# Waits of two output projections taken per pair, and two weight chunks summed earlier, in a two-block transformer kernel on one core

## The reference

```python
# first block
merged = jnp.einsum('bsnd,nbsd->bsd', gates, branch)
x = x + merged @ w_out[layer]                      # output projection, 512x1024 @ 1024x1024
# second block
h = rms_norm_2(x, norm_mix[l])
proj = h @ w_in[l]                                 # input projection, 6 strips of 392 columns, and gates
u, q, kc, vc, ksl, vsl, kwn, vwn, g_nsa, g_merge = jnp.split(proj, IN_SPLITS, axis=-1)
...                                                # compress(kc), compress(vc), pooling, sparse attention
merged = g_a * (y_pool @ w_proj_pool[l]) + g_b * (y_nsa @ w_proj_nsa[l])
x = x + merged @ w_out[l]                          # output projection
h = rms_norm_2(x, norm_mlp[l])
x = x + jnp.square(jax.nn.relu(h @ w_ff1[l])) @ w_ff2[l]
```

## Time and profile before

| | before |
|---|---|
| median of 3 runs | 1459.08 us (1457.42 to 1463.24) |
| profiled execution, own time | 1459.08 us |
| its span | 1457.3 us |
| PE busy | 1421.2 us, 98% |
| PE weight load busy | 1187.6 us, 81% |
| DVE / ACT / POOL busy | 61% / 46% / 42% |
| granted TensorE clock, mean | 0.998 |
| DMA | 170.30 MB, mean 117 GB/s |

### The profile page before, as it was taken

One profiled execution on the slowest core, in us unless ns is written; L12 is line 12 of the kernel. 1 busy time (PEld: TensorE's weight loads), 2 busy tenths in 40 slices (PEclk: granted clock), 3 DMA queues, 4 the chain that ended last, 5 costly groups with the idle time before them and its releaser, 6 DMA issues.

```text
span 1457.3 us, 20968 instructions
## 1 busy us (share of the span) xinstructions
PE 1421.2 (98%) x7693; PEld 1187.6 (81%) x7693; DVE 882.9 (61%) x1646; ACT 665.8 (46%) x1176; POOL 616.1 (42%) x433
## 2 busy tenths in 40 slices
PE   8999999989989999999999999999999999999998
PEld 7888888768778888889997777788888888888886
DVE  4336978465654276652555777772164777777776
ACT  5453645557564233343343666773235433223342
POOL 4333744344343445254433265563425333333330
PEclk9999999999999999999999999999999999999999
DMA  6222433203101666769662210004365433333321
GB/s 207 83 83 84 143 95 98 60 12 93 44 2 48 205 203 233 267 197 325 232 235 73 73 30 1 2 2 145 98 215 179 159 102 101 101 101 104 97 86 58
DMA packets 89115, 170.30 MB, mean 117 GB/s; under 512 B 7032, under 2 KB 31171, under 8 KB 89027
## 3 DMA queue, kind: packets, MB, share of 16 engines
q1 hardware_dynamic: 79298, 140.72, 30.7%
q10 hardware_dynamic: 9728, 28.39, 5.4%
HBM read 148.12 MB, written 20.97 MB: 116 GB/s over the span
## 4 chain that ended last, share of the span: by engine, by line
PE 91%; DVE 3%; ACT 2%; issue 2%; DMA 1%; POOL 1%; POOLq 0%; SPq 0%; DVEq 0%; ACTq 0%
PE bank L1015 58%; PE bank L1700 9%; PE bank L1276 4%; PE bank L1077 4%; PE bank L1284 4%; PE bank L1107 4%; PE bank L938 3%; PE bank L975 1%; PE bank L1109 1%; PE bank L1688 1%; DVE xt_lo L2953 1%; PE bank L1518 0%; PE bank L1227 0%; DMA raw<-in_w_in 0%; DVE prob_t L2765 0%
## 5 line engine op out<-in xcount | busy, mean ns | idle before, releaser
L774 POOL TENSOR_TENSOR w_lo<-raw,w_hi 128x1024 fp32r<-128x1024 f32 (+3 forms) x185 | 439.5, 2386 | 496.0 <-ACT w_hi L1776 495.7
L1776 ACT ACTIVATE w_hi<-raw 128x1024 fp32r<-128x1024 f32 (+3 forms) x189 | 191.4, 1015 | 367.5 <-DMA raw<-in_w_in 175.0
L1015 PE MATMUL bank<-xt_hi,w_hi 128*128 128x512 f32 x560 | 221.2, 395 | 0.0
L1015 PE MATMUL bank<-xt_hi,w_lo 128*128 128x512 f32 x560 | 218.2, 390 | 0.0
L1015 PE MATMUL bank<-xt_lo,w_hi 128*128 128x512 f32 x560 | 218.1, 389 | 0.0
L1015 PE MATMUL bank<-w_hi,xt_hi 128*128 128x484 f32 (+2 forms) x520 | 192.1, 369 | 0.0
L1015 PE MATMUL bank<-w_lo,xt_hi 128*128 128x484 f32 (+2 forms) x520 | 190.2, 366 | 0.0
L1015 PE MATMUL bank<-w_hi,xt_lo 128*128 128x484 f32 (+2 forms) x520 | 190.1, 366 | 0.0
L1015 PEld LDWEIGHTS bank<-xt_hi,w_hi 128*128 128x128 f32 x560 | 105.2, 188 | 23.4 <-issue 2.2
L1015 PEld LDWEIGHTS bank<-xt_hi,w_lo 128*128 128x128 f32 x560 | 105.1, 188 | 22.2
L1015 PEld LDWEIGHTS bank<-xt_lo,w_hi 128*128 128x128 f32 x560 | 105.2, 188 | 21.6 <-issue 0.5
(11 more groups left out here) (453 smaller groups left out, 2957.9 us busy)
## 6 DMA issues: line engine op xcount, KB each, us to landing
raw<-in_w_in SPq DMA_DIRECT2D x40, 512.0 KB, 3.6
raw<-in_w_in SPq DMA_DIRECT2D x40, 484.0 KB, 3.5
raw<-in_w_ff SPq DMA_DIRECT2D x36, 512.0 KB, 3.7
quarter_b<-in_w_ff SPq DMA_DIRECT2D x28, 512.0 KB, 3.5
raw<-in_w_in SPq DMA_DIRECT2D x24, 392.0 KB, 3.8
w_hi<-sums_hi SPq DMA_DIRECT2D x16, 512.0 KB, 4.9
w_lo<-sums_lo SPq DMA_DIRECT2D x16, 512.0 KB, 5.8
raw<-in_w_branch SPq DMA_DIRECT2D x12, 512.0 KB, 3.8
```

Source lines behind the costliest of these rows:

```text
L774: pool.tensor_tensor(w_lo[:, slot, 0:halves, 0:width], raw[:, slot, 0:halves, 0:width], w_hi[:, slot, 0:halves, 0:width].bitcast(F32), ALU ...
L1015: ins = pe.matmul(o, lhs, rhs, start=st and j == 0, stop=en and j == 2)
L1776: act.activation(w_hi[:, slot, 0:halves, 0:width], raw[:, slot, 0:halves, 0:width], ACT.Copy)\
```

## The change

Two edits.

In `out_products` the three terms of a pair are written inside the loops over its two row blocks and two banks. All waits of the pair stand ahead of its first matmul: both parts of the weights, both parts of the activations. `high_made`, `low_made`, `high_landed` and `low_landed` become `wait_pair` and `wait_sums`.

In the second block's input projection the steps of the chunks 5, 6 and 7 are moved. On ACT the high part and the stores of chunk 5 come before `empty_in2(2)`, those of chunk 6 before `empty_in2(3)`, the load of 7 before `next_hi(I + 21)`, and its high part behind `hidden_turned`. On DVE chunk 5 comes before the groups `ck` and `cv`, and chunk 6 before the gate signals.

```diff
@@ out_products
-                        for j, (rows, whole) in enumerate(((rows_hi, w_hi), (rows_lo, w_hi), (rows_hi, w_lo))):
-                            if j == 0:
-                                high_landed(p) if m in OF_SUMS else high_made(p)
-                            if j < 2 and m in (1, 4):
-                                pe.wait_ge(sem[("mhi", "mlo")[j]], 4 * n + (m == 4) * 2 + q + 1)
-                            if j < 2 and m in S_ORDER:
-                                pe.wait_ge(sem[("sums_hi", "sums_lo")[j]], 4 * n + S_ORDER.index(m) + 1)
-                            if j == 2:
-                                low_landed(p) if m in OF_SUMS else low_made(p)
-                            for kk in range(2):
-                                for u in range(2):
...
+                        if m in OF_SUMS:
+                            wait_sums(p)
+                        else:
+                            wait_pair(p)
+                        if m in (1, 4):
+                            pe.wait_ge(sem["mhi"], 4 * n + (m == 4) * 2 + q + 1)
+                            pe.wait_ge(sem["mlo"], 4 * n + (m == 4) * 2 + q + 1)
+                        for kk in range(2):
+                            wh, wl = w_hi[:, p % RING, kk, :], w_lo[:, p % RING, kk, :]
+                            for u in range(2):
+                                c = slice(u * P, u * P + P)
+                                lh, ll = rows_hi[:, 2 * q + kk, c], rows_lo[:, 2 * q + kk, c]
+                                for j, (lhs, rhs) in enumerate(((lh, wh), (lh, wl), (ll, wh))):
+                                    ins = pe.matmul(bank[OUT_BANK[m] + u][:], lhs, rhs,
...
@@ ACT, input projection of the second block
             for q in range(11, 15):
                 next_hi(I + q, IN2_W)
+                if q in (12, 13):
+                    (chunk_high if q == 12 else chunk_store)(5)
             empty_in2(2)
...
-            chunk_high(5)
             next_hi(I + 15, IN2_W)
+            chunk_load(6)
...
+            for q in range(16, 19):
+                next_hi(I + q, IN2_W)
+                if q in (17, 18):
+                    (chunk_high if q == 17 else chunk_store)(6)
             empty_in2(3)
             next_hi(I + 19, IN2_W)
             next_hi(I + 20, IN2_W)
-            chunk_high(6)
-            chunk_store(6)
+            chunk_load(7)
             next_hi(I + 21, IN2_W)
             hidden_tanh()
-            chunk_load(7)
...
             next_hi(I + 23, IN2_W)
+            hidden_turned()
             chunk_high(7)
-            hidden_turned()
@@ DVE
             whole_chunk(4)
+            whole_chunk(5)
             for k, (name, pe_col) in enumerate((("ck", VEC["pek"]), ("cv", VEC["pev"]))):
...
-            whole_chunk(5)
...
+            whole_chunk(6)
             dve.wait_ge(sem["tanh_out"], 1)
...
-            whole_chunk(6)
```

More of the change, by code:

```diff
@@ L1037, in turn_x, with wait_sums @@
                     .then_inc(sem["x_turned"], 1)
-            def high_landed(p):
-                pe.wait_ge(landed[p % RING], p // RING * 16 + 16)
-            def low_landed(p):
-                pe.wait_ge(landed_lo[p % RING], 16 * sum(t <= p and t % RING == p % RING for t in SUM_PAIRS))
+            def wait_sums(p):
+                slot = p % RING
+                pe.wait_ge(landed[slot], p // RING * 16 + 16)
+                pe.wait_ge(landed_lo[slot], 16 * sum(t <= p and t % RING == slot for t in SUM_PAIRS))
             def out_products(n, s, p0):
@@ L1057, in out_products @@
                     if m in S_ORDER:
+                        pe.wait_ge(sem["sums_hi"], 4 * n + S_ORDER.index(m) + 1)
+                        pe.wait_ge(sem["sums_lo"], 4 * n + S_ORDER.index(m) + 1)
                         k = S_ORDER.index(m)
@@ L1064, in out_products @@
                         p = p0 + 2 * i + q
-                        slot = p % RING
-                        for j, (rows, whole) in enumerate(((rows_hi, w_hi), (rows_lo, w_hi), (rows_hi, w_lo))):
-                            if j == 0:
-                                high_landed(p) if m in OF_SUMS else high_made(p)
-                            if j < 2 and m in (1, 4):
-                                pe.wait_ge(sem[("mhi", "mlo")[j]], 4 * n + (m == 4) * 2 + q + 1)
-                            if j < 2 and m in S_ORDER:
-                                pe.wait_ge(sem[("sums_hi", "sums_lo")[j]], 4 * n + S_ORDER.index(m) + 1)
-                            if j == 2:
-                                low_landed(p) if m in OF_SUMS else low_made(p)
-                            for kk in range(2):
-                                for u in range(2):
-                                    ins = pe.matmul(bank[OUT_BANK[m] + u][:], rows[:, 2 * q + kk, u * P:u * P + P], whole[:, slot, kk, :],
+                        if m in OF_SUMS:
[12 more added lines that the diff above has]
+                                    ins = pe.matmul(bank[OUT_BANK[m] + u][:], lhs, rhs,
                                                     start=m in (1, 7, 4, 6) and q == 0 and kk == 0 and j == 0,
```

11 lines of the change are left out of this document (1 added, 10 removed).

## The result

The changed kernel takes 1469.28 us (median of 8 runs, 1465.67 to 1470.86), the kernel before 1461.65 (8 runs beside it, 1457.42 to 1465.42). The ratio is 1.0052 with a 95% interval of 1.0038 to 1.0067: **slower by 0.5%**, 5.6 to 9.8 us. Forecast were 1464.9 us and 5.8 us of loss, with a range up to 1469.0: the direction held, the loss is larger, and the time lies just outside the range.

The account below looks back on a forecast made before the run. PE was taken to bound the kernel. Projections 1.1, chunk 5 standstill 3.6, clock 1.4, strip 3 stores 0 and gate strip -0.3 sum to 5.8 us on 1459.08, giving 1464.9 us; range 1461 to 1469.

Parts of the forecast that it names:

- What bounds the kernel: Whole kernel: PE is busy 98% of the span, so each microsecond PE stands still is a microsecond of time.
- Product 2: Both output projections: PE waits for POOL's low part of the weights, 0.7 us in the first, 0.4 in the second.
- Loads of sums: Output projections: loads awaited at the head of their pair still land in time, by 0.7 us; cost nothing.
- Chunk 5 ahead of the groups: Before strip 3: DVE finishes groups ck and cv at 700.2, PE comes at 696.62; 3.6 us of standstill.
- my allowance for the landing: Chunk 5's loads: a microsecond allowed for the landing, giving 2.6 us of standstill at the short end.
- The collision: Chunk 5's fourth add on DVE meets POOL's pair 12 low part: all 1.5 us later, 1466.4 us; chance 0.20.
- The clock: Behind the standstill at strip 3: PE's granted clock falls, costing 1.4 us, bounds nothing and 2.8.
- the rival without a fall: Strip 3: the clock doesn't fall, everything else as forecast, 1463.5 us; chance 0.22.
- Strip 3 behind the stores of chunk 6: ACT empties strip 3 after those stores: costed at nothing; rival 1.6 us more, 1466.5 us, chance 0.06.
- Gate strip: PE's 1.14 us wait at 760.90 may shrink: -0.3 us, between -1.1 and +0.5.
- Pay-back: PE's later waits, 760 to 850 us, shrink by up to 4.0 us and the clock stays: 1459.8 us; chance 0.07.
- The base: Starting time: the profiled execution's 1459.08 us, taken also as the median of the runs.

Follow-up runs that it names:

- e2: Kernel before with only the moved chunk steps on ACT and DVE, products as before: 1468.46 us, ratio 1.0042.
- e8: Kernel before with only chunk 7's loads ahead of pair 21's high part and the hidden layer turned ahead of chunk 7's high part: 1459.26 us, ratio 0.9985.
- e10: e7 with chunk 5's loads issued one pair earlier on ACT: 1462.72 us, ratio 1.0016 against the kernel before.
- e11: e8 with chunk 5's loads issued one pair earlier: 1459.41 us, ratio 0.9986 against the kernel before.
- e13: Kernel before, unchanged, profiled once more: 1462.79 us.
- e15: Kernel before, unchanged, another profile: 1458.97 us.
- e5: e2 with 18 extra matmuls of 512 columns on PE ahead of the wait for group cv: 1466.44 us, ratio 1.0036 against the kernel before.
- e1: Kernel before with only the edit of the output projections, chunks as before: 1461.52 us, ratio 1.0001.
- e4: Kernel before with its order of matmuls, but all waits of each projection pair at its head: 1461.28 us, ratio 1.0001.
- e12: e8 with the changed products of the output projections: 1461.61 us, ratio 1.0001 against the kernel before.
- e7: e2 with only the low part of chunk 5 moved behind groups ck and cv on DVE: 1464.40 us, ratio 1.0018 against the kernel before.
- e9: e2 with chunk 5's loads issued one pair earlier on ACT: 1469.55 us, ratio 1.0046 against the kernel before.
- e6: e2 with chunk 5's high part ahead of pair 12's on ACT: 1467.57 us, ratio 1.0041 against the kernel before.
- e3: e2 with all of DVE's chunk 5 behind groups ck and cv again: 1469.91 us, ratio 1.0057 against the kernel before.
- e14: Kernel before, unchanged, another profile: 1459.60 us.

## Why the prediction was wrong in size and right in direction

*What bounds the kernel*: right. Every microsecond of PE's standstill came back in the span; the table adds up without another term.

*Product 2*: the place and the releaser were right, the size was not. 0.7 and 0.4 us became 1.5 and 1.2, and with what PE loses around a wait 1.4 and 1.5 between the marks: 2.9 for the forecast's 1.1, over its bound of 1.5. POOL's low part was done at 623.77 + 4.74 / 2 = 626.14, as long as forecast for one (2.4), but it began 1.0 us later than in the earlier trace rows while PE came at 624.6, much as before. I had worked the margin out to tenths from one execution. In seven others with the old products (e2, e8, e10, e11, e13 to e15) the low part began 20.0 to 21.7 us after the start of the first projection, where mine had 20.75, and 19.5 to 21.4 after that of the second, where mine had 19.95; in the kernel after it was 21.4 and 20.9.

*Loads of sums*: right, no wait on them.

*Chunk 5 ahead of the groups*: **this is the step that failed.** Of "PE comes at 696.62: 3.6 us of standstill" the chain and its order were right: from the first add to the end of the groups the forecast has 13.2 us, and e5, where no add was slow, took 13.1. Wrong, by 2.4 us together, were the date on which the chain starts and the length of one link. The adds began 0.8 us later relative to PE: issued at 683.12, the loads landed as soon after issue as forecast, but the issue stood 15.2 us before PE was through, where the earlier trace rows have 16.3. And the fourth add met POOL, 1.6 us. 3.6 + 0.8 + 1.6 = 6.0, the measured standstill. The issue date can be followed in eight executions with this load in its old place and no standstill there: from it to the rows turned behind strip 3 (703.00 before) it was 22.6 us in the profile I worked from, and 20.7 to 22.3 in e1, e4, e8, e12 to e15. Mine was the one with most slack of all, and my allowance for the landing went the other way, to 2.6 us. e7 and e10 show the link itself: take the low part out of the chain and 4.0 us of standstill go; date the load earlier as well and none is left.

*The collision*: had as a rival of 0.20, exclusive of the forecast. The Trainium skill's rule (SBUF — State Buffer, "Who interferes with whom") names exactly this, and the runs agree: the fourth add took 2.26 to 2.28 us where POOL's low part had begun first (after, e2, e7, e9), and 0.69 where the add had begun first (e5, e10) or POOL's wasn't beside it (e6). The error was in the list of rivals: the collision, the clock and a late load can come together, as they did, and the range took the collision without a late load. Its upper end is 9.9 us; measured in the profile were 2.9 + 6.0 + 2.4 - 0.4 = 10.9, and 0.3 from ahead of the change.

*The clock*: it fell, as forecast (the rival without a fall is out for the kernel after). 1.4 us was mis-sized; strip 3 lost 2.4, near the upper bound of 2.8, since PE ran at 1.2 GHz for 5.1 us and not for the 3.1 us that I had taken from the program's start. That source was weaker than I made it: the matmuls of the start are slow, but the profile has a granted clock of 1.00 in that stretch, so that its end only, with 0.61, agrees by the clock. And the fall came at about 702.6, 4.3 us after PE stopped, not 2.0.

*Strip 3 behind the stores of chunk 6*: nothing, right for this order; e3 shows that it was near.

*Gate strip*: -0.3 forecast, -0.4 measured (wait 0.77 for 1.14). In the four traces of the kernel before this wait was 1.07 to 2.11 us, so that the size fits to a tenth is luck in part.

*Pay-back*: none of the later waits shrank beyond that.

*The base*: 1459.08 was a run of the lower group, and I called it the median of the runs, which it was, of three. The medians of 8 to 32 runs are 1461.65 to 1463.18, with the groups nearly even. Against the lower group's 1459.5 the change costs 9.8 us, against a median of both 7.6. The forecast sum of 5.8 was worked out from a profile of the lower group and was short by 4.0 us there; against the median of both it looks nearer than it was.

## What to carry to other kernels

Before an order is changed for the sake of one engine, list for each moved step whose work now stands behind it and on what date its input comes; a step that needs a load, another engine and itself in turn (load, sum, high, low) is to be moved only as far as nothing awaited stands behind its last link. Take that date from several executions: here it moved by 2 us with no edit at all. And look at the timed runs one by one before trusting a median: here they lay in two groups 4 us apart, in the profiled case by a fall of the clock behind one short wait, and the smallest piece of the change, which thins out the upper group, was the only one worth having.

## What the runs showed of the hardware

The granted clock fell behind short standstills of PE even when PE was already back at work: behind 2.6 us of idleness (e7, at strip 3) it fell 1.3 us after PE's return, behind 2.1 (e13, at the gate strip) 0.2 us after, behind 1.5 (e11, there) 1.7 us after. It didn't fall behind 2.0 (e10, there, and e3, at 703.48), nor behind 1.6 (e15) and 1.5 (e7) at the gate strip. What a fall cost didn't follow the idle time: 2.4 us after 5.9, 1.65 after 2.6, and at the gate strip, with the same instructions behind, 3.2 after 2.1 (e13) and 1.6 after 1.5 (e11), each by the time from the strip's first group to its second.

Where DVE's fourth add and POOL's low part met, the one that began later was slowed: DVE's add of 128x512 took 2.27 us for 0.69 when it began 0.14 us behind POOL's low part, and POOL's low part 2.08 for 1.87 when it began 0.36 us behind the add (e5).

A load of raw weights landed so that its high part started at the same 758.36 in two executions (e13, e14) in which PE's date differed by 1.0 us, so being early upstream gave nothing there.
